# A two-block fp32 model on one core: the first block's start, its memory keys and its early experts in another order

## What is computed

```python
h = rmsnorm(x, attn_norm_g)
proj = h @ w_in                                  # 1024 x 3072
a = diff_attention(...)                          # 4 heads, rotated queries and keys
r = retention(...)                               # 4 heads, two directions, group norm, silu gate
x = x + concat(a, r) @ w_out                     # 1024 x 1024
x = x + peer_ffn(rmsnorm(x, ffn_norm_g), ...)

def peer_ffn(xb):
    q = xb @ w_query                             # 8 heads x 2 halves x 128
    s = q . sub_keys                             # 128 scores for each half
    top 16 of each half, 16 best of their 256 sums -> eid, gate
    act = gelu(expert_down[eid] . xb)            # 16384 = 128 x 128 experts
    return sum over eid of gate * act * expert_up[eid]
```

## Time and profile before

| | us |
|---|---|
| runs | 1678.34, 1673.07, 1686.61 (median 1678.34) |
| the profiled execution | 1679.54, of which span 1677.7 |
| PE busy | 1531.7 (91% of the span) |
| PEld busy | 1376.6 (82%) |
| POOL busy | 998.3 (59%) |
| DVE busy | 815.2 (49%) |
| ACT busy | 758.6 (45%) |
| mean granted TensorE clock | 0.958 |

### The profile page before, as it was taken

How to read it: one execution, slowest core, us unless ns; L and a number is a source line. 1 busy time by engine, 2 the same in 40 slices (tenths; PEclk the granted TensorE clock), 3 DMA queues, 4 the chain that set the end, 5 groups by cost and what they waited for, 6 DMA issues and landing times.

```text
span 1677.7 us, 26777 instructions
## 1 busy us (share of the span) xinstructions
PE 1531.7 (91%) x9622; PEld 1376.6 (82%) x9622; DVE 815.2 (49%) x2040; ACT 758.6 (45%) x1234; POOL 998.3 (59%) x425
## 2 busy tenths in 40 slices
PE   6996999899999999999999999689978977799996
PEld 5675998799988889999999999579767766599995
DVE  4555599989965552222222222336775312155554
ACT  6456544444444544444444444555335443444443
POOL 6544878645530018888888888478420452568884
PEclk9998999899999999999999999799987988889998
DMA  6433557433336656565565665455320342335652
GB/s 221 126 101 113 165 163 227 150 102 114 114 116 198 190 187 187 188 188 187 185 186 185 185 186 190 149 167 183 101 76 13 133 120 74 113 126 188 182 184 96
DMA packets 68700, 254.09 MB, mean 151 GB/s; under 512 B 7680, under 2 KB 7680, under 8 KB 67728
## 3 DMA queue, kind: packets, MB, share of 16 engines
q1 hardware_dynamic: 66816, 243.82, 46.5%
q10 hardware_dynamic: 1296, 6.82, 1.1%
q0 software_dynamic: 512, 2.45, 0.4%
HBM read 249.91 MB, written 3.15 MB: 151 GB/s over the span
## 4 chain that ended last, share of the span: by engine, by line
PE 37%; issue 28%; POOL 23%; DVE 9%; ACT 2%; POOLq 1%; DVEq 0%; ACTq 0%
POOL w_lo L395 23%; PE bank L426 11%; PE bank L427 11%; PE bank L428 11%; PE bank L754 4%; DVE arena L1917 1%; DVE arena L1914 1%; PE bank L1081 1%; DVE xres L1695 1%; DVE arena L1916 1%; DVE arena L1915 1%; DVE h_lo L1668 1%; ACT arena L1186 1%; DVE arena L1985 1%; DVE arena L1983 1%
## 5 line engine op out<-in xcount | busy, mean ns | idle before, releaser
L395 POOL TENSOR_TENSOR w_lo<-ring,w_hi 128x1024 fp32r<-128x1024 f32 x415 | 994.7, 2399 | 657.1 <-ACT w_hi L1148 649.0
L1148 ACT CAST w_hi<-ring 128x1024 fp32r<-128x1024 f32 x460 | 482.7, 1050 | 715.8 <-PE bank L428 687.3
L426 PE MATMUL bank<-h_hi,w_hi 128*128 128x256 f32 x1696 | 487.7, 288 | 7.8 <-DVEq L374 5.7
L427 PE MATMUL bank<-h_lo,w_hi 128*128 128x256 f32 x1696 | 481.7, 284 | 0.0
L428 PE MATMUL bank<-h_hi,w_lo 128*128 128x256 f32 x1696 | 481.6, 284 | 0.0
L426 PEld LDWEIGHTS bank<-h_hi,w_hi 128*128 128x128 f32 x1696 | 327.0, 193 | 13.3 <-DVEq L374 6.9
L427 PEld LDWEIGHTS bank<-h_lo,w_hi 128*128 128x128 f32 x1696 | 327.2, 193 | 3.9
L428 PEld LDWEIGHTS bank<-h_hi,w_lo 128*128 128x128 f32 x1696 | 326.7, 193 | 0.0
L426 PE MATMUL bank<-w_hi,act_hi 128*128 128x512 f32 x600 | 236.3, 394 | 5.2 <-DVE act_lo L2044 4.0
L427 PE MATMUL bank<-w_lo,act_hi 128*128 128x512 f32 x600 | 235.7, 393 | 0.0
L428 PE MATMUL bank<-w_hi,act_lo 128*128 128x512 f32 x600 | 234.4, 391 | 0.0
(11 more groups left out here) (343 smaller groups left out, 1880.9 us busy)
## 6 DMA issues: line engine op xcount, KB each, us to landing
ring<-weights_in SPq DMA_DIRECT2D x463, 512.0 KB, 3.5
mem_kv<-arena ACTq DMA_DIRECT2D x2, 1024.0 KB, 6.8
arena<-mem_kv ACTq DMA_DIRECT2D x2, 1024.0 KB, 6.0
xres<-x_in SPq DMA_DIRECT2D x1, 1024.0 KB, 4.9
arena<-mem_in POOLq DMA_DIRECT2D x1, 1024.0 KB, 11.2
arena<-rows_in ACTq DMA_DIRECT2D x2, 512.0 KB, 4.3
out<-arena ACTq DMA_DIRECT2D x1, 1024.0 KB, 3.9
arena<-consts_in POOLq DMA_DIRECT2D x1, 512.0 KB, 11.8
```

The costliest lines, as they stand in the source:

```text
L395: nc.gpsimd.tensor_tensor(w_lo[:, k, :], ring[:, k, :], w_hi[:, k, :].bitcast(F32), ALU.subtract)\
L426: pe.matmul(out_, a[0], b[0], start=start, stop=False, **kw)
L427: pe.matmul(out_, a[0], b[1], start=False, stop=False, **kw)
L1148: nc.scalar.copy(w_hi[:, k, :], ring[:, k, :]).then_inc(s["hi_made"], 1)
```

## The change

1. **Start.** PE transposes x as it is, not divided by its norm, the first 128 tokens when they have landed, then the other 128. The factor 1/rms of a token comes in later, when the product with `w_in` is copied out of PSUM (L1230 and L1757 become a multiplication by `rstd`, and the silu gets it as its scale). The sums of squares are made after the cuts. SP loads slot 0 first, then x in two halves. `cst` and `cols` are loaded from ACT's queue. POOL makes the `w_lo` of slot 0 first and then issues the other four loads. Each load has its own semaphore.
2. **Memory keys.** The 8 `mem_k` slots move from behind the queries to right behind `w_out`. DVE adds the first 128 tokens when their half of the last `out_slot` is made. ACT and DVE make the norm beside the first four `mem_k` slots, PE transposes behind the fourth, ACT and DVE cut beside the last four. The two barriers are gone. ACT runs a square root on one column (`warm_1`) ahead of it, so that the table of the square root is loaded.
3. **Experts.** `E_FIRST` = 28: 28 `down`s stand ahead of the choice, 60 `up`s follow the rounds, 68 experts are left. Some areas of SBUF move, since the gates of 28 experts now lie where keys and lists were.

```diff
-E_FIRST, CHUNKS, GROUPS = 16, 4, T // 4
+E_FIRST, CHUNKS, GROUPS = 28, 4, T // 4
 EARLY = E_FIRST + GROUPS * CHUNKS // KD
 LATE = NK - EARLY
...
-    order = ["w_in", "w_out", "queries", "mem_k", "mem_v", "experts", "dt_q", "kv_rope", "z", "xbc", "q_up", "kv_up",
+    order = ["w_in", "w_out", "mem_k", "queries", "mem_v", "experts", "dt_q", "kv_rope", "z", "xbc", "q_up", "kv_up",
...
+FIRST_AT = [(4, 0), (5, 0), (6, 0), (7, 0), (2, 0), (2, T), (3, 0), (3, T)]
...
-            sp.dma_start(xres[:, :, :], x_in).then_inc(s["x_loaded"], 16)
-            for n in range(N_SLOTS):
+            sp.dma_start(ring[:, 0, :], weights[SOURCE[0]]).then_inc(loaded[0], 16)
+            sp.dma_start(xres[:, 0, :], x_in[:, 0, :]).then_inc(s["x_loaded"], 16)
+            sp.dma_start(xres[:, 1, :], x_in[:, 1, :]).then_inc(s["x_rest_loaded"], 16)
+            for n in range(1, N_SLOTS):
...
-            pool.dma_start(cols[:, :], cols_in).then_inc(s["params_loaded"], 16)
-            pool.dma_start(cst[:, :], consts[:, 0:NCONST]).then_inc(s["params_loaded"], 16)
-            pool.dma_start(rows[:, :], rows_in[:, 0:NROWS]).then_inc(s["params_loaded"], 16)
-            pool.dma_start(pos_i[:, :], pos_in).then_inc(s["params_loaded"], 16)
+            lo_part(0, 0)
+            pool.dma_start(rows[:, :], rows_in[:, 0:NROWS]).then_inc(s["rows_loaded"], 16)
             pool.dma_start(mem[:, :, :], mem_in).then_inc(s["mem_loaded"], 16)
-            pool.dma_start(area("later_earlier"), consts[:, NCONST:NCONST + 1024]).then_inc(s["params_loaded"], 16)
-            lo_parts(0, DVE_FIRST)
+            pool.dma_start(area("later_earlier"), consts[:, NCONST:NCONST + 1024]).then_inc(s["later_loaded"], 16)
+            pool.dma_start(pos_i[:, :], pos_in).then_inc(s["pos_loaded"], 16)
+            lo_parts(1, DVE_FIRST)
...
-            pe.wait_ge(s["params_loaded"], 80)
-            norm_turn("attn_norm", NORMS["attn"], bank0=4)
+            def first_turn():
+
+                pe.wait_ge(s["ident_loaded"], 16)
+                pe.wait_ge(s["x_loaded"], 16)
+                for t in range(TT):
+                    if t == 1:
+                        pe.wait_ge(s["x_rest_loaded"], 16)
+                    for b in range(KD):
+                        to, c = FIRST_AT[b]
+                        mm = pe.transpose(bank[:, to, c + t * P:c + (t + 1) * P], xres[:, t, b * P:(b + 1) * P], ident)
+                        if t == 1:
+                            mm.then_inc(s["turned"], 1)
+
+            first_turn()
...
+                    if k == KD - 1 and t == 0:
+                        mm.then_inc(s["mixer_half"], 1)
...
-            end(pe)
-
-            begin(pe, 1)
-            norm_turn("ffn_norm", NORMS["ffn"])
-            end(pe)
-
-            begin(pe, 2)
+
+            low("mem_b", 3)
+            for j in range(8):
+                n = STEP["mem_k"] + j
+                if j >= 2:
+                    pe.wait_ge(s["copied_act"], COPY["mem_k"][0] + j - 1)
+                wait_slot(pe, n)
+                for k in range(KD):
+                    mm = product(bank[:, 4 + j % 2, 0:T], both(w_parts, every, n % NS, slice(k * P, (k + 1) * P)),
+                                 both(mem_t, every, k, slice(0, T)), start=(k == 0), stop=(k == KD - 1))
+                mm.then_inc(s["spent"], 1)
+                if j == 3:
+                    pe.wait_ge(s["mixer_added"], 2 * TT)
+                    pe.wait_ge(s["norm_scaled"], SCALED["ffn"])
+                    turn("ffn_norm", lambda b, t: x_scaled[:, t, b * P:(b + 1) * P], KD)
+            low("ffn_norm", KD - 1)
+            pe.wait_ge(s["copied_act"], COPY["mem_k"][0] + 8)
...
-            for j in range(8):
-                n = STEP["mem_k"] + j
-                if j >= 3:
...
-            act.wait_ge(s["x_loaded"], 16)
-            norm(NORMS["attn"], xres)
+            act.dma_start(cst[:, :], consts[:, 0:NCONST]).then_inc(s["ident_loaded"], 16)
+            act.dma_start(cols[:, :], cols_in).then_inc(s["cols_loaded"], 16)
+            hi_parts(1)
+            act.wait_ge(s["cols_loaded"], 16)
+            for b in range(KD):
+                to, c = FIRST_AT[b]
+                last = max(i for i in range(KD) if FIRST_AT[i][0] == to)
+                act.wait_ge(s["turned"], TURN["attn_norm"][0] + last + 1)
+                nc.scalar.mul(h_t[0][:, b, :], bank[:, to, c:c + T], col("attn_g", b)).then_inc(s["split_act"], 1)
+                if b == 1:
+                    hi_parts(2)
             hi_parts(NS)
-            act.wait_ge(s["params_loaded"], 80)
-            turned_hi("attn_norm", h_t, KD, lambda b: col("attn_g", b), bank0=4)
+            norm_sums(NORMS["attn"], xres)
+            hi_parts(NS + 1)
+            act.wait_ge(s["norm_mean"], NORMS["attn"] + 1)
+            nc.scalar.activation(rstd[:, 0:2], ssq[:, 2:4], ACT.Sqrt).then_inc(s["norm_rooted"], 1)
...
-                hi_parts(NS + 1 + t)
+                hi_parts(NS + 2 + t)
...
-                nc.scalar.copy(proj[:, 0, c * 512:(c + 1) * 512], bank[:, 2 * (c % 2), :]).then_inc(s["copied_act"], 1)
+                if c == 0:
+                    act.wait_ge(s["norm_factor"], NORMS["attn"] + 1)
+                nc.scalar.mul(proj[:, 0, c * 512:(c + 1) * 512], bank[:, 2 * (c % 2), :], rstd[:, 2:3]).then_inc(s["copied_act"], 1)
...
-            hi_parts(STEP["w_out"] + KD + NS)
-            end(act)
-            begin(act, 1)
-            norm(NORMS["ffn"], xres)
-            turned_hi("ffn_norm", h_t, KD, lambda b: col("ffn_g", b))
-            end(act)
-            begin(act, 2)
+            nc.scalar.activation(warm_1[:, :], ident[:, 0:1], ACT.Sqrt)
+            hi_parts(STEP["w_out"] + KD - 1 + NS)
+            mem_k_at = STEP["mem_k"]
+
+            def mem_k_copied(j):
+                act.wait_ge(s["spent"], mem_k_at + j + 1)
+                nc.scalar.copy(mk_first[:, j, :], bank[:, 4 + j % 2, 0:T]).then_inc(s["copied_act"], 1)
+
+            for t in range(TT):
+                act.wait_ge(s["mixer_added"], 2 * t + 2)
+                nc.scalar.activation(squares, xres[:, t, :], ACT.Square, accum_out=ssq[:, t:t + 1]).then_inc(s["norm_summed"], 1)
+                act.wait_ge(s["norm_summed"], 2 * NORMS["ffn"] + t + 1)
+                hi_parts(mem_k_at + NS + t)
+            act.wait_ge(s["norm_mean"], NORMS["ffn"] + 1)
+            nc.scalar.activation(rstd[:, 0:2], ssq[:, 2:4], ACT.Sqrt).then_inc(s["norm_rooted"], 1)
+            mem_k_copied(0)
+            act.wait_ge(s["norm_factor"], NORMS["ffn"] + 1)
+            nc.scalar.mul(x_scaled[:, 0, :], xres[:, 0, :], rstd[:, 2:3]).then_inc(s["norm_scaled"], 1)
+            for j in range(1, 4):
+                hi_parts(mem_k_at + j + 1 + NS)
+                mem_k_copied(j)
+            turned_hi("ffn_norm", h_t, 4, lambda b: col("ffn_g", b))
+            hi_parts(mem_k_at + 5 + NS)
+            mem_k_copied(4)
+            turned_hi("ffn_norm", h_t, 4, lambda b: col("ffn_g", 4 + b), first=4, skip=4)
+            for j in range(5, 8):
+                hi_parts(mem_k_at + j + 1 + NS)
+                mem_k_copied(j)
...
-            for j in range(8):
...
-                if k == E_FIRST // 2:
+                if k == E_FIRST - 8:
...
-            dve.wait_ge(s["x_loaded"], 16)
-            norm(NORMS["attn"], xres)
-            dve.wait_ge(s["params_loaded"], 80)
-            turned_lo("attn_norm", h_t, KD, lambda b: col("attn_g", b), bank0=4)
+            dve.wait_ge(s["cols_loaded"], 16)
+            for b in range(KD):
+                to, c = FIRST_AT[b]
+                last = max(i for i in range(KD) if FIRST_AT[i][0] == to)
+                dve.wait_ge(s["split_act"], SPLIT["attn_norm"] + last + 1)
+                v.scalar_tensor_tensor(out=h_t[1][:, b, :], in0=bank[:, to, c:c + T], scalar=col("attn_g", b), in1=h_t[0][:, b, :].bitcast(F32),
+                                       op0=ALU.mult, op1=ALU.subtract).then_inc(s["lo_made"], 1)
...
-            into_residual(STEP["w_out"] + 8)
-            end(dve)
-            begin(dve, 1)
+            for t in range(TT):
+                if t == 0:
+                    dve.wait_ge(s["mixer_half"], 1)
+                else:
+                    dve.wait_ge(s["spent"], STEP["w_out"] + KD)
+                for h in range(2):
+                    v.tensor_tensor(xres[:, t, h * 512:(h + 1) * 512], xres[:, t, h * 512:(h + 1) * 512],
+                                    bank[:, 2 * t + h, :], ALU.add).then_inc(s["mixer_added"], 1)
+            dve.wait_ge(s["mixer_added"], 2 * TT)
             norm(NORMS["ffn"], xres)
             turned_lo("ffn_norm", h_t, KD, lambda b: col("ffn_g", b))
-            end(dve)
-            begin(dve, 2)
...
-            dve.wait_ge(s["copied_act"], COPY["mem_k"][0] + 8)
```

113 lines of the change are left out of this document (61 added, 52 removed).

## The result

The changed kernel takes 1670.3 us in the median of its runs (1664.5 to 1674.3) against 1680.05 for the kernel before (1673.1 to 1686.6) beside it: a ratio of 0.9944, 95% interval 0.9931 to 0.9958. It is faster, but by 0.56% where 1.2% was forecast, and outside the range of 1651 to 1668. The profiled execution went from a span of 1677.7 us to 1666.9.

A forecast was written before the change was run, and what follows sets the result against it. PE, busy 91% of the span, bounds the kernel; the first block gains only what PE loses by standing or low clock. 6 + 10.1 - 2.4 + 8.1 - 1 - 0.3 = 20.5 us, median about 1658, range 1651 to 1668.

The forecast's parts named there:

- The start: Up to the first slots: first product near 9.5 instead of 19.2, of which 6 us stay; bounds 9.7 and 2.
- the rival of a late start: The start gives next to nothing, ACT having too much between its casts: gain 2 there, total 1662; chance 0.2.
- the one slower than before: At the start `mem` lands late on POOL's queue and holds up ACT's casts: 1697 if at 60; chance 0.03.
- The end of the mixer: From T, PE's end of `w_out`, to the queries: 28.8 us with the memory keys inside, a gain of 10.1.
- the forecast's reason for taking nothing for it: Mixer's norm: two full POOL cuts put the division at T + 13.3, ahead of PE's asking at T + 13.9.
- Behind the keys: Ahead of `mem_v`, which waits until all keys are copied, without the memory keys as cover: 2.4 us lost.
- The choice: PE's wait for DVE goes (5.4), transposes get cheaper (0.8), low clock behind them goes (1.9): gain 8.1.
- The 1 us taken off for the clock there: Behind the choice: the remaining wait of 2.79 may bring the low clock back; 1 us off.
- Spread to ups: The rounds: DVE's L2029 grows by 48 columns, 3 us against 9.9 of idle time; 0.3 off, 3 at worst.
- the moved experts cost nothing: Experts moved ahead of the choice change nothing by themselves: `down` and `up` 5.61 us together, 5.63 in the last loop.
- Each new stop costs the low clock: Four stops of 1.5 to 3 us; three more low clocks at 1.9 each take 6: 1664; chance 0.12.

The follow-up runs named there:

- start_only: The kernel before with the new start alone (undivided x, tables on their own queues, slot 0 ahead of x): 1672.08 us, ratio 0.9957.
- fill: The changed kernel with 41 matmuls that nobody reads in PE's two stops at the keys, the waits kept: 1665.27 us, ratio 0.9911.
- stops_covered: The changed kernel with five stops of PE attacked by order and finer waits, without useless matmuls: 1658.56 us, ratio 0.9876.
- no_key_stops: The changed kernel with later parts of the choice on DVE and `mem_v`'s wait split, against the two stops at the keys: 1667.28 us, ratio 0.9915.

## Why the prediction was wrong

**The start, forecast 6, measured 3.6 at T, 5.35 at the marker of the scores.** The order of ACT's chain was right, its times 0.3 to 1.5 us early: casts forecast at 8.9, 12.5, 16.0, 19.9, 22.1 and 27.1 start at 10.35, 13.44, 16.79, 20.68, 22.68 and 27.36. Too early was the landing of x, forecast 6.1, measured 7.36, with 362 GB/s between 3 and 15 us instead of the 397 of before; the first product is at 10.84, not 9.5. `mem` landed 9.0 us from its issue and nobody waited for it, so the rival of a late start and the one slower than before had nothing to stand on. Slot 6, forecast whole at 30.5, is whole at 30.9. The rest is the low stretch at 128.6, 1.6 by its window, behind a stop of 2.17 us that the kernel before has too, without one. Where the new start runs without that stretch, T comes at 144.95 to 145.09 (start_only, fill, stops_covered), 5.5 to 5.6 us earlier than before: so the start was worth nearly its 6, and by these kernels 2.0 of the miss is the clock and 0.4 the late landing. ACT's timeline:

```profile
16.79 1.05 ACT L1169 CAST w_hi<-ring 128x1024 fp32r<-128x1024 f32 x1
20.68 1.05 ACT L1169 CAST w_hi<-ring 128x1024 fp32r<-128x1024 f32 x1 [0.28 <-DMA ring<-weights_in]
27.36 1.04 ACT L1169 CAST w_hi<-ring 128x1024 fp32r<-128x1024 f32 x1
```

**The end of the mixer, forecast 28.8 from T to the queries, measured 30.4.** The stops are as forecast: 2.60 behind `w_out`, released by POOL (2.4), no wait ahead of the ffn transposes, 1.51 ahead of the queries (1.5). The 1.6 too much is the low stretch behind the first of them, which the sum had left out. DVE's division of x did wait for a cut of POOL, 2.71 us at 155.44; the forecast's reason for taking nothing for it, that PE asks later, held.

**Behind the keys, forecast a loss of 2.4, measured 7.4.** This is the step that failed. The stop itself was right, 2.16 us, released by ACT. But I took the memory keys out of this place at 24.6 us and put `mem_v` behind the last keys as if it ran as before. The memory keys had not only covered a wait, they had brought PE back to full clock after the stop of 3.0 us ahead of the last keys: full work at once, and 3.4 us of low clock (6.8 in start_only). With them gone, a second stop follows 5.4 us behind the first, and the clock stays low for 13.7. Fill shows it: with work in both stops the line is 87.1, and the whole of the miss is gone. Fillings in one of the two stops alone were not tried; no_key_stops, which has no second stop and a shorter first one, had 6.8 us of low clock.

**The choice, forecast a gain of 8.1.** PE no longer waits for it and comes 10.5 us behind DVE (forecast 7; 5 of low clock are in it). The six transposes take 0.82 (0.7). The wait behind them is 3.50, not 2.79, since ACT is busy with the last downs when it should copy the chosen. The 1 us taken off for the clock there was nearly right, 1.4. DVE's chain took 162.3 us from the queries, forecast 161. Spread to ups, where the rounds got 48 columns more, came as forecast (154.5 against 154.4), and the moved experts cost nothing (565.4 against 565.7).

**Which rival it was.** "Each new stop costs the low clock", given 0.12 and 1664. Its mechanism is what happened; its size was wrong, since 1.9 us a stop is the price of a lone one. Against it stood the stop of 2.16 ahead of 274.11 with full clock behind it: one instance, taken for a rule. Sum: some 8.2 of the 9.7 us that the span lacks are low clock (1.6, 1.6 and 5.0) and 0.7 the longer wait behind the choice. Work in the stops has shown this for the 5.0; for the two stretches of 1.6 it is read from the windows. The 0.8 left over I put to the later x, which is a remainder and not a measurement; by the kernels without the stretch at 128.6 it is 0.4, and the clock's part 8.6.

## What to carry to other kernels

A stop of TensorE has two prices, its length and the clock behind it, and work that is moved away from behind a stop takes with it what had brought the clock back: look at what follows each remaining stop, above all at two stops with a short piece of work between. Put waits apart from each other or lay real work over them (a transposition two steps earlier, a wait split by banks); where nothing real is to be had, matmuls that nobody reads, cut to the length of the stop, gave 5 us in two stops and 11.6 in seven; in three stops, two of them ahead of DVE's choice, they gave 2.9, not clear of noise, and in one long stop nothing. And what one engine wins should be costed at its next hand-over: in the two fastest kernels without work in every stop, PE stood 3.8 and 4.7 us for DVE's choice.
